# Two transformer blocks in one kernel: ScalarE's order at the block boundaries, and two gate units in the attention's last tiles

## The chip, the cores and the metric

The kernel runs on one core of a Trainium2 chip. The metric is device time in microseconds for one execution of the whole program. Three executions of the kernel before were timed; one further execution was profiled.

## The reference

Two blocks run one after the other on x of 256 tokens by 1024 channels, all in float32. The first is sparse and windowed attention beside a gated MLP, followed by a SwiGLU feed-forward. The second is a block with adaptive modulation: latent attention over chosen keys beside a state-space mixer (SSD), then a SwiGLU feed-forward.

```python
# first block
h = h + rms_norm(mixer(rms_norm(h, norm_mix_pre)), norm_mix_post)
h = h + rms_norm(swiglu_ffn(rms_norm(h, norm_ffn_pre)), norm_ffn_post)
# second block
mod = (silu(c) @ ada_w + ada_b)             # six rows of 1024: shift, scale and gate, twice
h = rmsnorm(x, pre_norm_mix) * (1.0 + scale_m) + shift_m
proj = h @ w_in                             # q_lat, kv_lat, k_idx, w_idx, z, xbc, dt, g_a, g_b
y_a = sparse_mla_attention(...) @ w_o_attn  # 16 heads, latent keys of 128
y_b = ssd_mixer(z, xbc, dt_raw, ...) @ w_o_ssd
mix = (sigmoid(g_a) * y_a + sigmoid(g_b) * y_b) @ w_out
x = x + gate_m * rmsnorm(mix, post_norm_mix)
h2 = rmsnorm(x, pre_norm_ffn) * (1.0 + scale_f) + shift_f
x = x + gate_f * rmsnorm((silu(u_gate) * u_up) @ w_ffn_out, post_norm_ffn)
```

## The kernel before

Every matrix product of float32 is made of three products of rounded parts: high times high, high times low, low times high. A weight unit of 128 partitions by 1024 numbers is loaded by SyncE into a ring of RING = 4 slots (`w_raw`). ScalarE copies it to its high part (`w_hi`, L870, in `split`), VectorE subtracts to get its low part (`w_lo`, L1357), and for some units GpSimd does the subtraction (L715). TensorE takes the units in order. `split_to(u)` on ScalarE or VectorE means: split all units up to u that are not split yet. A slot's high part can be rewritten once TensorE has used the unit before it (`unit_used`). All five queues are written out by hand, each engine works strictly in its own order, and semaphores tie them together.

The streams of weights that matter here, in order: `s_wo` (output of the first mixer), `s_gu` (first feed-forward, in), `s_dn` (its output), `s_lat` (latents of the second block), `s_z`, `s_z2` (z of the SSD), `s_ga` (gate g_a, 8 units), `s_oa` (attention output, 8 units), `s_xbc` (input of the convolution, 16 blocks of two units), and later `s_wo2`, `s_gu2`, `s_dn2`.

**The boundaries.** Between two parts x is updated and normalised again; there are three of them, `boundary(0)` after `s_wo`, `boundary(1, 0)` after `s_dn` and `boundary(2, 1)` after `s_wo2`. A product is made in two column halves. The last four units of the second half are done for token half 0 first, then for token half 1, so that token half 0 can be worked on meanwhile. For each token half t:

- ScalarE squares the product's halves (`square_m0` at L898, `square_m1` at L909) and takes the root (`root_m` at L913); the root needs a table load, which the one-column activation into `warm` (L959) brings forward.
- VectorE multiplies with the gain (`gained`, L1403), updates x (`new_x`, L1413), multiplies x with the next gain (`gain_x`, L1420).
- ScalarE squares x and takes the root (`square_x`, L920 to L924); VectorE makes a diagonal of the reciprocal (`rstd_x`, L1397 and L1398).
- TensorE turns x with that diagonal (`turn`, L2102, 8 products into banks 4 to 7).
- ScalarE reads the turned x in four pieces as high parts of h (`piece_hi`, L932 without a shift, L936 with one), VectorE makes the low parts (`piece_lo`, L1357 or L1432), and TensorE begins the next product for that token half, piece by piece (L2061 to L2063, or L2428 for the latents).

Four units of each next stream (v, v+1, v+2, v+3) are held in buffers of their own, since they are used once for each token half. The low part of v+3 is made by GpSimd, of the others by VectorE.

**The second attention.** It runs over NTILE = 32 tiles of 8 queries. Step n of the loop on TensorE makes the logits of tile n (L2493 to L2498), transposes the weights of tile n-2 (L2506), makes single pieces of z (`s_z2`, until step 24), and multiplies with the values for tile n-3 (L2520). In the last three steps only the latter parts are left. z's blocks are read on ScalarE by `read_z` (L1215), at steps 17 and 33. Behind the loop follow the per-head output matmuls (L2527), the cumulated sums for the SSD (L2534 to L2538), the gate's units into banks 0 to 3, and the attention output into banks 4 to 7:

```python
        pe.wait_ge(act_read, s_z2.act0 + s_z2.n)
        for c in range(2):
            if c == 1:
                pe.wait_ge(uv_lo, 2)
            for j in range(4):
                u = s_ga.u0 + 4 * c + j
                pe.wait_ge(lo_ready, u + 1)
                for t in range(TT):
                    ins = tm_half(u, 2 * j, t, bank[2 * c + t][:, :], h_hi, h_lo, j == 0, j == 3)
                ins.then_inc(unit_used, 1)
```

Through the gate's and the output's units VectorE also does `modulate`: 24 steps (L1481, L1484) that add silu(c) times a row block of `ada_w` (chunks 7 to 9 of 8 steps each) to an accumulator. GpSimd loads those rows by quarters of a chunk (L724), beginning when the per-head output matmuls are done; a quarter is loaded when VectorE has used the same quarter of the chunk before. TensorE sums the accumulators over partitions (`add_up`, L2152), ScalarE copies the sums (L1259), and GpSimd stores them (`store_sums`) and waits for the landing, between two low parts of `s_xbc` that it makes.

Of the kernel before, what the change touches and what calls it, by code (L numbers as in the profile page):

```python
# [26 lines left out]
ACT = mybir.ActivationFunctionType  # L27
# [4 lines left out]
TT = S // P  # L32
# [83 lines left out]
def _emit(nc, ctx, a, out):  # L116
# [418 lines left out]
    GB_READ = (4, 13)  # L535
    OS_STEPS = {KI - 2: 2, KI - 1: 2, KI: 4, KI + 1: 4}
# [310 lines left out]
    def _(act):  # L847
# [92 lines left out]
        def product_end(b):  # L940

            st = PRODUCTS[b]
            split_to(st.u0 + len(st.ks) + 3)
            square_m0(b, 0)
            split_to(st.u0 + len(st.ks) + 4)
            square_m0(b, 1)
            split_to(st.u0 + 2 * len(st.ks))

        def boundary(b, bias=None):
# [9 lines left out]
            act.activation(warm[:, 2 + b:3 + b], eps, ACT.Sqrt)  # L959
# [4 lines left out]
            if b != 1:  # L964
                square_m1(b, 1)
                root_m(b, 1)
            piece_hi(b, 0, 0, bias)
            piece_hi(b, 0, 1, bias)
            if b == 1:
                square_m1(b, 1)  # L970
                root_m(b, 1)
            split_to(v + 4)
# [252 lines left out]
        for n in range(NTILE + 2):  # L1225
# [16 lines left out]
            if n % 16 == 1 and n > 16:  # L1242
                read_z(s_z2, n // 16 - 1, 2 + 2 * s_z.n + 2 * (n // 16 - 1))
# [14 lines left out]
        act.wait_ge(sums_mm, 2)  # L1258
        act.activation(sums2[0:96, 0, :], bank[2][0:96, :], ACT.Copy).then_inc(sums_read, 1)  # L1259
        for b in range(s_xbc.n + 1):  # L1260
            if b < s_xbc.n:
# [85 lines left out]
    def _(dve):  # L1347
# [430 lines left out]
        for n in range(NTILE + 4):  # L1778
# [18 lines left out]
            if n % 8 in (2, 3) and n < NTILE:  # L1797
                split_half(s_z2.u0 + n // 8 + AHEAD, n % 8 - 2)
        for b in range(4):
# [17 lines left out]
        for b in range(4):  # L1817
            split_to(s_ga.u0 + 2 * b + 2 + AHEAD)
# [120 lines left out]
    def _(pe):  # L1939
# [546 lines left out]
        z2_tile = 0  # L2486
        for n in range(NTILE + 3):
# [21 lines left out]
            for _ in range(2 if n < 2 else 1 if n % 2 == 0 and z2_tile < 2 * KD else 0):  # L2509
# [3 lines left out]
                z2_tile += 1  # L2513
            if n >= 3:
# [7 lines left out]
                ins.then_inc(lt_pv, 1)  # L2522
        pe.wait_ge(uv_in, 16)
# [16 lines left out]
        pe.wait_ge(act_read, s_z2.act0 + s_z2.n)  # L2540
        for c in range(2):
            if c == 1:
                pe.wait_ge(uv_lo, 2)
            for j in range(4):
                u = s_ga.u0 + 4 * c + j
                pe.wait_ge(lo_ready, u + 1)
                for t in range(TT):
                    ins = tm_half(u, 2 * j, t, bank[2 * c + t][:, :], h_hi, h_lo, j == 0, j == 3)
                ins.then_inc(unit_used, 1)
# [11 lines left out]
        add_up(MOD_FIRST, MOD_SECOND, 2)  # L2561
        for b in range(2):
            fm_block(s_xbc, b, h_hi, h_lo)
        with pe.Fori(1, s_xbc.n // 4) as i:
# [145 lines left out]
```

## Time and profile before

| what | value |
|---|---|
| median of 3 runs | 956.2 us (955.8 to 957.12) |
| the profiled execution | 954.68 us |
| its span, first to last instruction | 953.0 us |
| TensorE busy | 938.7 us, 98% |
| VectorE busy | 662.6 us, 70% |
| ScalarE busy | 539.8 us, 57% |
| GpSimd busy | 233.6 us, 25% |
| read from HBM | 176.90 MB, 187 GB/s over the span |
| granted TensorE clock | 1.000 |

The difference between the profiled execution's time and its span (1.7 us) lies before the first and after the last instruction. Boundary 0 lies at 125 to 150 us of the span, boundary 1 at 321 to 344, the second attention at 416 to 484, the gate's and the attention output's units at 490 to 534, the convolution from 535 on, boundary 2 at 745 to 768. Idle time of an engine stands in brackets in a timeline, with what ended it; a busy TensorE is not one at its peak, since the ends of matmuls are modelled.

### The profile page before, as it was taken

The numbers are of one execution on the slowest core, as the hardware profiler recorded it, in microseconds if no ns is written. First come the engines' busy times: TensorE is split into PE (matmuls) and PEld (weight loads), VectorE is DVE, ScalarE is ACT, GpSimd is POOL, SyncE is SP. The second block draws the span as 40 slices with busy tenths as digits, with TensorE's granted clock in tenths as the row PEclk, the third lists the DMA queues.
The fourth block names the chain that finished last, engine by engine and source line by source line (L and its number), as shares of the span: only waits on it lengthen the run. The fifth ranks groups of instructions, "written<-read, shape, count | busy, mean of one in ns | idle before, by whom it ended". The sixth has DMA issues, their size and how long they took to land.

```text
span 953.0 us, 15383 instructions
## 1 busy us (share of the span) xinstructions
PE 938.7 (98%) x5665; PEld 801.9 (84%) x5665; DVE 662.6 (70%) x1098; ACT 539.8 (57%) x958; POOL 233.6 (25%) x235
## 2 busy tenths in 40 slices
PE   9999999999999999999999999999999999999997
PEld 8987887888887898999978899986688878888786
DVE  5776676777786668965678666678976767755453
ACT  6677675444535558744546456567764664544443
POOL 5304001111122150499922144320200101000100
PEclk9999999999999999999999999999999999999999
DMA  9765268788888714750149666651345778666561
GB/s 284 236 185 167 80 195 267 243 277 274 276 298 243 234 46 132 201 154 23 29 164 338 181 184 189 163 172 67 111 155 165 232 243 259 189 190 189 192 219 67
DMA packets 131352, 179.00 MB, mean 188 GB/s; under 512 B 8124, under 2 KB 96910, under 8 KB 131280
## 3 DMA queue, kind: packets, MB, share of 16 engines
q1 hardware_dynamic: 120384, 144.53, 48.3%
q0 software_dynamic: 10304, 33.18, 11.5%
q8 instruction: 44, 0.72, 0.3%
q10 hardware_dynamic: 592, 0.34, 0.1%
q14 instruction: 28, 0.23, 0.1%
HBM read 176.90 MB, written 1.12 MB: 187 GB/s over the span
## 4 chain that ended last, share of the span: by engine, by line
PE 86%; DVE 5%; ACT 5%; DMA 2%; issue 1%; POOL 1%; SPq 0%; DVEq 0%; ACTq 0%; POOLq 0%
PE bank L2061 17%; PE bank L2063 17%; PE bank L2062 16%; PE bank L1982 16%; PE bank L2497 1%; PE bank L2493 1%; PE bank L2520 1%; DVE w_lo L1357 1%; PE bank L2234 1%; PE bank L2013 1%; DMA w_raw<-in_w_in 1%; PE bank L2428 1%; PE bank L2116 1%; ACT w_hi L870 1%; PE bank L2102 1%
## 5 line engine op out<-in xcount | busy, mean ns | idle before, releaser
L1357 DVE TENSOR_TENSOR w_lo<-w_raw,w_hi 128x1024 fp32r<-128x1024 f32 (+1 forms) x243 | 284.5, 1192 | 75.8 <-ACT w_hi L870 75.3
L870 ACT ACTIVATE w_hi<-w_raw 128x1024 fp32r<-128x1024 f32 (+1 forms) x262 | 265.8, 1038 | 113.9 <-PE bank L2063 74.3
L2061 PE MATMUL bank<-w_hi,h_hi 128*128 128x512 f32 x448 | 179.0, 399 | 0.2 <-DVE h_lo L1357 0.2
L2063 PE MATMUL bank<-w_hi,h_lo 128*128 128x512 f32 x448 | 174.8, 390 | 0.0
L2062 PE MATMUL bank<-w_lo,h_hi 128*128 128x512 f32 x448 | 174.3, 389 | 0.0
L1982 PE MATMUL bank<-h_hi,w_hi 128*128 128x256 f32 x432 | 124.5, 288 | 1.4 <-DVE h_lo L1520 1.1
L1982 PE MATMUL bank<-h_lo,w_hi 128*128 128x256 f32 x432 | 122.1, 283 | 0.0
L1982 PE MATMUL bank<-h_hi,w_lo 128*128 128x256 f32 x432 | 122.1, 283 | 0.0
L2061 PE MATMUL bank<-w_hi,ff_hi 128*128 128x512 f32 x272 | 107.6, 395 | 0.3
L2062 PE MATMUL bank<-w_lo,ff_hi 128*128 128x512 f32 x272 | 106.0, 390 | 0.0
L2063 PE MATMUL bank<-w_hi,ff_lo 128*128 128x512 f32 x272 | 105.9, 389 | 0.0
L2063 PEld LDWEIGHTS bank<-w_hi,h_lo 128*128 128x128 f32 x448 | 84.1, 188 | 18.0
L2061 PEld LDWEIGHTS bank<-w_hi,h_hi 128*128 128x128 f32 x448 | 84.2, 188 | 16.2 <-issue 0.6
L2062 PEld LDWEIGHTS bank<-w_lo,h_hi 128*128 128x128 f32 x448 | 84.3, 188 | 15.8
L715 POOL TENSOR_TENSOR w_lo<-w_raw,w_hi 128x1024 fp32r<-128x1024 f32 x27 | 65.2, 2414 | 117.7 <-DVE w_lo L1357 94.2
L1982 PEld LDWEIGHTS bank<-h_hi,w_hi 128*128 128x128 f32 x432 | 82.7, 192 | 3.1 <-DVE w_lo L1357 1.5
L1982 PEld LDWEIGHTS bank<-h_lo,w_hi 128*128 128x128 f32 x432 | 82.8, 192 | 0.0
L1982 PEld LDWEIGHTS bank<-h_hi,w_lo 128*128 128x128 f32 x432 | 82.7, 191 | 0.0
L724 POOL DMA_DIRECT2D ada_raw<-in_ada_w x48 | 34.4, 718 | 188.3 <-DVE ada_acc L1484 175.6
L1484 DVE SCALAR_TENSOR_TENSOR ada_acc<-ada_raw,c_silu,ada_acc 128x512 f32<-128x512 f32 x84 | 63.0, 750 | 4.0 <-DVE ada_acc L1484 0.5
L816 POOL TENSOR_SCALAR ff_hi<-pos_f,own_pos 128x256 fp32r<-128x256 f32 x64 | 64.2, 1018 | 3.5 <-PE bank L2498 3.5
L997 ACT ACTIVATE silu_tok<-bank 128x256 f32<-128x256 f32 x44 | 16.9, 384 | 81.5 <-PE bank L2063 81.4
(463 smaller groups left out, 1634.3 us busy)
## 6 DMA issues: line engine op xcount, KB each, us to landing
w_raw<-in_w_in SPq DMA_DIRECT2D x84, 512.0 KB, 3.8
ada_raw<-in_ada_w POOLq DMA_DIRECT2D x48, 512.0 KB, 6.2
w_raw<-in_w_gate_up SPq DMA_DIRECT2D x88, 256.0 KB, 5.2
w_raw<-in_w_ffn_in SPq DMA_DIRECT2D x88, 256.0 KB, 3.9
w_raw<-in_w_down SPq DMA_DIRECT2D x22, 512.0 KB, 6.3
w_raw<-in_w_ffn_out SPq DMA_DIRECT2D x22, 512.0 KB, 4.3
w_raw<-in_w_out SPq DMA_DIRECT2D x16, 512.0 KB, 3.7
w_raw<-in_w_o_ssd SPq DMA_DIRECT2D x16, 512.0 KB, 3.5
```

The costliest lines, as they stand in the source:

```text
L715: pool.tensor_tensor(low(u, n), w_raw[:, u % RING, 0:n], high(u, n).bitcast(F32), ALU.subtract).then_inc(lo_ready, 1)
L724: pool.dma_start(ada_raw[:, j, :].rearrange("p (k c) -> p k c", k=2), ada[:, 2 * j:2 * j + 2, 512 * MOD_CHUNKS[c]:512 * MOD_CHUNKS[c] + 51 ...
L816: ins = pool.tensor_scalar(reached[:, n % 2, c, :], pos_f[:, 0:S], own_pos[:, 2 * n + c:2 * n + c + 1], None, ALU.is_ge)
L870: act.activation(high(u, n), w_raw[:, u % RING, 0:n], ACT.Copy).then_inc(hi_ready, 1)
L997: act.activation(silu_tok[:, b % 2, t, :], bank[2 * (b % 2) + t][:, 0:256], ACT.Silu).then_inc(gu_silu, 1)
L1357: return dve.tensor_tensor(dst, src, hi.bitcast(F32), ALU.subtract)
L1484: ins = dve.scalar_tensor_tensor(acc, src, c_silu[:, k:k + 1], acc, ALU.mult, ALU.add)
L1982: ins = pe.matmul(out_b[:, s, :], w[:, kk, c], x[:, k0 + k, :], start=k == 0 and s == 0 and step == 0, stop=k == sum(st.ks) - 1 and s == 1 ...
L2013: ins = pe.matmul(out_b[:, t, 0:ncol], x[:, k, c], w[:, kk, :], start=first, stop=end and last and t == 1, skip_group_check=True)
L2061: pe.matmul(out, x_hi[:, k, x], hi, start=start, stop=False, skip_group_check=True)
L2062: pe.matmul(out, x_hi[:, k, x], lo, start=False, stop=False, skip_group_check=True)
L2063: return pe.matmul(out, x_lo[:, k, x], hi, start=False, stop=stop, skip_group_check=True)
```

## The change

Eight edits are made.

1. In `product_end(0)`, on ScalarE, the activation into `warm` that loads the root's table stands before the unit `s_wo.u0 + 6`; the one in `boundary` remains for boundary 1 alone. (In boundary 2 the table is already the right one.)
2. In `boundary` on ScalarE the order is now the same for all three: squares of x for token half 0, the held unit v+3, pieces 0 and 1, square and root of token half 1, pieces 2 and 3. Before, boundaries 0 and 2 had square and root first, pieces 0 and 1, the held unit, pieces 2 and 3; boundary 1 had pieces 0 and 1, square and root, the held unit, pieces 2 and 3.
3. The second block of z is read at step 29 in place of step 33.
4. The gate's unit 0 is done in two halves, in steps 32 and 33 of the attention's loop, between the transposes and the values; its unit 1 directly behind the loop; the other six where all eight stood.
5. ScalarE and VectorE split the gate's units 2 and 3 before they read the per-head outputs.
6. VectorE splits two more units ahead of each group of three modulation steps in the gate's part.
7. TensorE does `add_up` of chunks 7 to 9 behind the first two blocks of `s_xbc`, in place of before them.
8. ScalarE copies these sums at the third turn of its convolution loop, in place of before the loop.

```diff
+    Z2_READ = (17, 29)
@@ ScalarE, product_end
+            if b == 0:
+                split_to(st.u0 + len(st.ks) + 2)
+                act.activation(warm[:, 2:3], eps, ACT.Sqrt)
             split_to(st.u0 + len(st.ks) + 3)
@@ ScalarE, boundary
             split_to(v + 2)
-            act.activation(warm[:, 2 + b:3 + b], eps, ACT.Sqrt)
+            if b == 1:
+                act.activation(warm[:, 3:4], eps, ACT.Sqrt)
             square_m1(b, 0)
             root_m(b, 0)
             split_to(v + 3)
             square_x(b, 0)
-            if b != 1:
-                square_m1(b, 1)
-                root_m(b, 1)
+            split_to(v + 4)
             piece_hi(b, 0, 0, bias)
             piece_hi(b, 0, 1, bias)
-            if b == 1:
-                square_m1(b, 1)
-                root_m(b, 1)
-            split_to(v + 4)
+            square_m1(b, 1)
+            root_m(b, 1)
             piece_hi(b, 0, 2, bias)
@@ ScalarE, second attention
-            if n % 16 == 1 and n > 16:
-                read_z(s_z2, n // 16 - 1, 2 + 2 * s_z.n + 2 * (n // 16 - 1))
+            if n in Z2_READ:
+                b = Z2_READ.index(n)
+                read_z(s_z2, b, 2 + 2 * s_z.n + 2 * b)
+        split_to(s_ga.u0 + 4)
@@ ScalarE, convolution
-        act.wait_ge(sums_mm, 2)
-        act.activation(sums2[0:96, 0, :], bank[2][0:96, :], ACT.Copy).then_inc(sums_read, 1)
         for b in range(s_xbc.n + 1):
+            if b == 2:
+                act.wait_ge(sums_mm, 2)
+                act.activation(sums2[0:96, 0, :], bank[2][0:96, :], ACT.Copy).then_inc(sums_read, 1)
@@ VectorE
+        split_to(s_ga.u0 + 4)
         for b in range(4):
             dve.wait_ge(uv_hi, b + 1)
@@ VectorE
-            split_to(s_ga.u0 + 2 * b + 2 + AHEAD)
+            split_to(s_ga.u0 + 2 * b + 4 + AHEAD)
             for step in range(3 * b, 3 * b + 3):
@@ TensorE
+        def ga_half(c, j, t):
+
+            u = s_ga.u0 + 4 * c + j
+            if t == 0:
+                pe.wait_ge(lo_ready, u + 1)
+            ins = tm_half(u, 2 * j, t, bank[2 * c + t][:, :], h_hi, h_lo, j == 0, j == 3)
+            if t == TT - 1:
+                ins.then_inc(unit_used, 1)
+
         for n in range(NTILE + 3):
@@ TensorE, between the transposes (and z) and the values of a step
+            if n in (NTILE, NTILE + 1):
+                if n == NTILE:
+                    pe.wait_ge(act_read, s_z2.act0 + s_z2.n)
+                ga_half(0, 0, n - NTILE)
@@ TensorE, behind the loop
+        for t in range(TT):
+            ga_half(0, 1, t)
         pe.wait_ge(uv_in, 16)
@@ TensorE, behind the cumulated sums
-        pe.wait_ge(act_read, s_z2.act0 + s_z2.n)
         for c in range(2):
             if c == 1:
                 pe.wait_ge(uv_lo, 2)
-            for j in range(4):
-                u = s_ga.u0 + 4 * c + j
-                pe.wait_ge(lo_ready, u + 1)
+            for j in range(2 - 2 * c, 4):
                 for t in range(TT):
-                    ins = tm_half(u, 2 * j, t, bank[2 * c + t][:, :], h_hi, h_lo, j == 0, j == 3)
-                ins.then_inc(unit_used, 1)
+                    ga_half(c, j, t)
@@ TensorE, convolution
-        add_up(MOD_FIRST, MOD_SECOND, 2)
         for b in range(2):
             fm_block(s_xbc, b, h_hi, h_lo)
+        add_up(MOD_FIRST, MOD_SECOND, 2)
```

## Rows read from the trace of the kernel before

**Rows 1.** The page: busy us, share of the span and count, first engines.

```profile
PE 938.7 (98%) x5665; PEld 801.9 (84%) x5665; DVE 662.6 (70%) x1098; ACT 539.8 (57%) x958; POOL 233.6 (25%) x235
```

**Rows 2.** TensorE's waits: us in total, times, longest.

```profile
PE bank L2102 <- DVE rstd L1398: 2.4, 3, 0.9
```

**Rows 3.** Timeline, boundary 0: start us, us, engine, what, idle before and its releaser.

```profile
125.03 1.06 ACT L870 ACTIVATE w_hi<-w_raw 128x1024 fp32r<-128x1024 f32 x1 [1.37 <-PE bank L2063]
...
131.83 2.36 DVE L1357 TENSOR_TENSOR ff_lo<-w_raw,ff_hi 128x1024 fp32r<-128x1024 f32 x2 [0.17 <-ACT ff_hi L870]
...
132.71 0.39 PE L2063 MATMUL bank<-w_hi,h_lo 128*128 128x512 f32 x1
...
132.76 1.28 ACT L959 ACT_TABLE_LOAD   x1
...
134.17 0.58 ACT L909 ACTIVATE var_sd<-bank 128x512 f32<-128x512 f32 x1
...
138.15 0.39 PE L2063 MATMUL bank<-w_hi,h_lo 128*128 128x512 f32 x1
...
139.25 2.02 PE L2102 MATMUL bank<-rstd,mT 128*128 128x128 f32 x16 [0.71 <-DVE rstd L1398]
...
141.88 2.38 POOL L715 TENSOR_TENSOR ff_lo<-w_raw,ff_hi 128x1024 fp32r<-128x1024 f32 x1 [44.27 <-ACT ff_hi L870]
...
142.93 1.90 DVE L1413 SCALAR_TENSOR_TENSOR x_tok<-mT,st,x_tok 128x512 f32<-128x512 f32 x1
...
147.65 2.02 PE L2102 MATMUL bank<-rstd,mT 128*128 128x128 f32 x16 [0.92 <-DVE rstd L1398]
```

**Rows 4.** Timeline, boundary 1.

```profile
332.78 1.14 ACT L936 ACTIVATE h_hi<-bank,shift 128x128 fp32r<-128x128 f32 x4 [1.38 <-PE bank L2102]
...
334.73 0.88 ACT L870 ACTIVATE lat_hi<-w_raw 128x832 fp32r<-128x832 f32 x1
...
336.91 0.35 PE L2428 MATMUL bank<-lat_hi,h_hi 128*128 128x256 f32 x1 [1.07 <-DVE h_lo L1432]
...
337.40 1.46 DVE L1413 SCALAR_TENSOR_TENSOR x_tok<-mT,st,x_tok 128x512 f32<-128x512 f32 x2
...
340.59 0.29 DVE L1398 TENSOR_SCALAR rstd<-mats,st 128x128 f32<-128x128 f32 x1
```

**Rows 5.** Timeline, boundary 2.

```profile
750.05 0.39 PE L2063 MATMUL bank<-w_hi,h_lo 128*128 128x512 f32 x1
...
750.47 0.60 ACT L909 ACTIVATE var_sd<-bank 128x512 f32<-128x512 f32 x1 [0.30 <-PE bank L2063]
...
756.84 1.12 ACT L936 ACTIVATE h_hi<-bank,shift 128x128 fp32r<-128x128 f32 x4
...
758.23 0.47 PE L2061 MATMUL bank<-ff_hi,h_hi 128*128 128x512 f32 x1 [0.38 <-DVE h_lo L1432]
...
760.69 1.25 DVE L1413 SCALAR_TENSOR_TENSOR x_tok<-mT,st,x_tok 128x512 f32<-128x512 f32 x1
...
764.77 2.02 PE L2102 MATMUL bank<-rstd,mT 128*128 128x128 f32 x16 [0.81 <-DVE rstd L1398]
```

**Rows 6.** Timeline of TensorE, the second attention's last tiles.

```profile
481.13 0.44 PE L2506 MATMUL bank<-mats,isc 128*128 128x128 f32 x2 [0.31 <-DVE isc L1789]
481.54 0.71 PE L2520 MATMUL bank<-work,kv 128*128 128x128 f32 x4
...
484.13 3.67 PE L2527 MATMUL bank<-oT,work 128*64 128x256 f32 x32 [0.47 <-DVE oT L1794]
```

**Rows 7.** The loads of ada_w and a pair of low parts; last, the loads' us to landing.

```profile
488.25 2.93 POOL L724 DMA_DIRECT2D ada_raw<-in_ada_w  x4 [9.45 <-PE bank L2527]
...
514.26 2.36 DVE L1357 TENSOR_TENSOR w_lo<-w_raw,w_hi 128x1024 fp32r<-128x1024 f32 x2 [2.10 <-ACT w_hi L870]
...
DMA to landing us min/median/max: 4.3/6.2/7.3
```

**Rows 8.** Timeline of TensorE in the convolution, a unit's first matmul.

```profile
561.08 0.38 PE L1982 MATMUL bank<-h_hi,w_hi 128*128 128x256 f32 x1
```

## The prediction, made before the changed kernel was run

> **What bounds the kernel now.** I read the page's busy times first: TensorE is busy 938.7 of 953.0 us [rows 1], so neither another engine nor the transfers can be what the whole kernel waits for; the change can only win what TensorE still loses in gaps. Then the list of TensorE's waits, longest in total first [rows 2]: on top is the turn of x at the boundaries (L2102), behind the diagonal that VectorE makes at L1398. Then the timeline around each boundary, around the end of the second attention, and through the gate's and the attention output's units. The ends of matmuls are modelled, so I go by starts: 24 matmuls of 512 columns, the second token half of a product, lie between 132.71 and 138.15, 0.227 us each [rows 3], and one is shown as 0.39 us long. A gap is therefore the idle time that the row shows plus 0.16 us: 0.71 + 0.16 = 0.87 us and 0.92 + 0.16 = 1.08 ahead of the two turns of boundary 0 [rows 3]; 1.07 + 0.16 = 1.23 inside boundary 1 [rows 4]; 0.38 + 0.17 = 0.55 ahead of 758.23 and 0.81 + 0.16 = 0.97 ahead of 764.77 in boundary 2 [rows 5].
>
> **Boundary 0, the root table.** The last matmul of the first token half starts at 132.71; ScalarE is then in the table load (132.76, 1.28 us), warms the table (0.1 us more, since it overlaps), and squares the half only at 134.17 [rows 3]. In boundary 2, whose table is in place, the same square starts 0.42 us after the same matmul (750.05 to 750.47) [rows 5]. With the load moved up it starts at 132.71 + 0.42 = 133.13. Not all of that 1.04 us reaches the turn: VectorE splits two units from 131.83 for 2.36 us [rows 3], and takes up the half only behind them; from 134.87, a short wait after the square, to 134.15. So the first turn comes 0.72 us earlier, at 138.5, with 0.15 us of gap left. The load now stands ahead of the unit whose high part starts at 125.03 after 1.37 us of idle time [rows 3]: load and warming are 1.4 us, so it slips by at most 0.1 us, and its low part, done at 127.4, is only reached around 130.2. Cost nothing; without that cover 1.4 us.
>
> **Boundaries 0 and 2, the held unit.** Its high part (1.05 us) and the square and root of the second half (1.02 us) change places; the unit now stands before the first pieces of h. There ScalarE is free: from the end of x's squares until the first transposes are through, 0.72 us after the turn begins (332.06 to 332.78 in boundary 1, 1.38 us idle [rows 4]). Boundary 0: free from 137.85, unit to 138.9, pieces at 138.5 + 0.72 = 139.2; nothing lost, and pieces 2 and 3 keep their place. Boundary 2: unit 755.15 to 756.2, pieces at 755.82 + 0.72 = 756.54 in place of 756.84, TensorE at 757.95 in place of 758.23 [rows 5]: 0.28 us.
> What matters more stands on GpSimd. It makes this unit's low part and starts when the high part is there: at 141.88, 2.38 us [rows 3], and in boundary 2 the same way. VectorE's first update of x falls inside it and takes 1.90 us (142.93) and 1.25 us (760.69); in boundary 1, hardly disturbed, two together take 1.46 us [rows 3 to 5]. After the change GpSimd runs at about 139.6 to 142.0 and 756.9 to 759.3 and is done before the update starts, at 142.5 and 760.4; what VectorE does in between reads PSUM and was not slower beside GpSimd before. From the update's start to a possible turn I take boundary 1: 337.40 to the diagonal's end at 340.88, and 0.15, make 3.6 us [rows 4]. Boundary 0: second turn at 142.5 + 3.6 = 146.1 in place of 147.65, 1.5 us in all, the first turn's share included (TensorE itself is ready at about 145.85). Boundary 2: 760.43 + 3.6 = 764.05 in place of 764.77, with everything 0.65 us. Bounds: if the update stays as slow, only 0.72 and 0.28 remain, less 0.1 for the later second square; above, the whole gaps, 1.95 and 1.5.
> The Trainium skill (SBUF — State Buffer, Who interferes with whom) gives a reason: a VectorE instruction with two SBUF inputs and a GpSimd one that reads SBUF exclude each other, and the later one blocks until the other ends. The trace agrees: the update of 142.93 ended at 144.83, 0.57 us after GpSimd at 144.26. By that rule the update runs at full speed once GpSimd is done, which is my sum; were the slowness of another kind, boundaries 0 and 2 would give 0.9 us together in place of 2.15.
>
> **Boundary 1.** Square and root stood between the pieces already, and the unit (0.88 us, 334.73) behind them, so that pieces 2 and 3 came late and TensorE stood still for 1.23 us [rows 4]. The unit goes into the 1.38 us before 332.78 and ends at 332.3. Pieces 2 and 3 start 0.8 us earlier, and TensorE with them. The diagonal of the second half moves along (340.88 to 340.1), ahead of TensorE's need at 340.45. 0.8 us; below 0.5, if some returns at the second turn; above 1.2.
>
> **The end of the second attention.** The last tiles leave gaps: 0.31 + 0.16 = 0.47 us at 481.13, which stays, since it is ahead of transposes behind which the new work stands; 0.47 + 0.17 = 0.64 us at 484.13; and, start to start, 0.14 us ahead of 481.54 and some 0.4 us in like pieces behind it [rows 6]. Four half units of 6 matmuls (1.36 us each, moved and not added) fill all but the first. Each change of kind costs about 0.1 us, so of 1.2 us I count 0.8; bounds 0.5 and 1.1. The bank needs z's last read, moved on ScalarE from behind the loop to step 29, where 0.6 us fits into the 0.96 us of idle time of a step; units 2 and 3 of the gate are split ahead of the attention's output, where both engines stood idle for 1.9 us.
>
> **What comes later.** The output matmuls (L2527) and the sums behind them start some 4.7 us later than before, and GpSimd's loads of ada_w wait for the former (488.25, now about 492.9) [rows 7]. VectorE finishes the cumulated parts at 498.0 in place of 493.3, but has two units fewer ahead. From there: a pair of units takes 2.28 us (514.26 to the steps behind it) [rows 7], three steps of modulation 2.3, a chunk's products with the gate 1.2. I walked that chain against TensorE's 2.72 us a unit from 494.8. Tightest: the output product's unit 4 (low part 521.4, wanted 522.0), unit 6 (527.0 against 527.5), and the first quarter of chunk 9 (landed about 522.7, wanted 523.4, by the median of 6.2 us to landing [rows 7]). Half a microsecond of slack each, so 0, and this is a rival below. The sums of the modulation move behind two blocks of the convolution: the same matmuls, no gain of their own, but GpSimd's queue (low parts, the store of the sums with a wait for its landing, low parts again) gets that much more room, and the gap at 561.08 goes, 0.34 us behind the start of the matmul before it where the pace is 0.12 [rows 8]. ScalarE's copy of the sums (0.6 us) now stands before the third block's splits, which are wanted 4 us later.
>
> **The sum.** 1.5 + 0.8 + 0.65 + 0.8 + 0.2 = 3.95 us. Behind each place TensorE sets its own pace and the others follow its marks, so nothing should swallow it. The profiled execution took 954.68 us for a span of 953.0; it would take 950.7. The median of the runs shown is 1.5 us above it: 956.2 - 4.0 = 952.2 us.
>
> **The rivals.** *Half of it* (0.20): the updates of x stay slow for another reason, or a second turn finds its next limit: 0.9 + 0.6 + 0.6 = 2.1 us, 954.1 us. *No change* (0.17): the gains come but are lost again in the tight chain on VectorE; a stall of 2 to 4 us there leaves 954.3 to 956.2, say 955.2. *Slower* (0.06): VectorE's backlog. It is in order; where it waits for a quarter of ada_w, the low parts behind wait too. A quarter is only loaded when the same quarter of the chunk before is used, so a start 4.7 us later and two loads in a row at the worst landing seen, 7.3 us in place of 6.2 [rows 7], put it late by up to 6.9 us. From 0.5 us on TensorE pays, from 4.5 us on the change loses; 6.9 us would give 956.2 - 4.0 + 6.4 = 958.6. Against it: VectorE had time to spare in that chain, 2.10 us at 514.26 alone [rows 7]. *More* (0.05): all gaps go, 6 us, 950.2.
>
> **How the numbers follow.** The likeliest case (0.52) is 952.2, with its own range 951.2 to 953.6. 0.2% is 1.9 us and about what a measurement tells from no change; faster is 0.52 + 0.20 + 0.05 = 0.77, same 0.17, slower 0.06. The range 950.8 to 955.0 leaves out the slower case, part of the unchanged one and the end of the larger gain.
>
> **What would show it.** Right: the first turn of boundary 0 within 0.2 us of the product's last matmul; all updates of x at L1413 near 0.75 us; no wait at L2428; between the last tiles only one gap, ahead of the transposes; no wait of L2061 for a low part through the attention output. Wrong: a gap near 1 us still ahead of the second turns; TensorE waiting for w_lo between 495 and 540 us, with VectorE idle behind ada_raw; the table load in the way of a split.

## The result, and the profile after

The changed kernel took 950.34 us (median of 6 runs, 949.83 to 950.92) beside 956.16 us for the kernel before (median of 6 runs on the same chip, 954.55 to 957.12): a ratio of 0.9942, with a 95% interval of 0.993 to 0.9953. It is faster, by more than the forecast said: 952.2 us was forecast, and the range began at 950.8. The profiled execution took 950.07 us for a span of 948.4 us, 4.6 us less than the span of before.

The page's busy line and the list of TensorE's waits, us in total, times and longest:

```profile
PE 937.6 (99%) x5665; PEld 801.2 (84%) x5665; DVE 659.5 (70%) x1098; ACT 539.0 (57%) x957; POOL 233.7 (25%) x235
```

```profile
PE bank L2163 <- POOL wsT L663: 1.1, 1, 1.1
PE bank L1987 <- DVE h_lo L1524: 0.9, 1, 0.9
PE bank L2107 <- DVE rstd L1402: 0.5, 2, 0.3
PE bank L2521 <- DVE isc L1793: 0.3, 1, 0.3
```

The turn of x, which stood on top of this list before [rows 2], now waits 0.5 us in place of 2.4 (L2107 is the same line as L2102 before). The two rows above it are of the kernel's first 12 us.

The timeline at boundary 0, to be read beside [rows 3]: first ScalarE's square, then both turns, GpSimd's subtraction and VectorE's pair of updates.

```profile
132.83 0.60 ACT L910 ACTIVATE var_sd<-bank 128x512 f32<-128x512 f32 x1 [0.39 <-PE bank L2068]
...
138.17 2.02 PE L2107 MATMUL bank<-rstd,mT 128*128 128x128 f32 x16
...
139.34 2.39 POOL L716 TENSOR_TENSOR ff_lo<-w_raw,ff_hi 128x1024 fp32r<-128x1024 f32 x1 [42.03 <-DVE ff_lo L1361]
...
141.80 1.41 DVE L1417 SCALAR_TENSOR_TENSOR x_tok<-mT,st,x_tok 128x512 f32<-128x512 f32 x2
...
145.49 1.95 PE L2107 MATMUL bank<-rstd,mT 128*128 128x128 f32 x16
```

Neither turn has an idle time in brackets (the 8 products of a turn show as 16 records). GpSimd is through at 141.73, 0.07 us before the updates begin, and two of them take 1.41 us where one took 1.90.

Boundary 1, beside [rows 4]: the second held unit of the latents on ScalarE, the table load behind it, the first turn, a product with the latents and the second turn. Boundary 2, beside [rows 5]: both turns. The end of the attention, beside [rows 6]: the transposes, and the per-head output matmuls.

```profile
322.86 1.06 ACT L871 ACTIVATE lat_hi<-w_raw 128x1024 fp32r<-128x1024 f32 x1 [1.58 <-DMA w_raw<-in_w_in]
323.94 1.28 ACT L964 ACT_TABLE_LOAD   x1
...
330.43 2.02 PE L2107 MATMUL bank<-rstd,mT 128*128 128x128 f32 x16 [0.26 <-DVE rstd L1402]
...
334.50 0.36 PE L2433 MATMUL bank<-lat_hi,h_hi 128*128 128x256 f32 x1 [0.28 <-DVE h_lo L1436]
...
338.66 1.96 PE L2107 MATMUL bank<-rstd,mT 128*128 128x128 f32 x16
...
478.67 0.44 PE L2521 MATMUL bank<-mats,isc 128*128 128x128 f32 x2 [0.31 <-DVE isc L1793]
...
486.09 3.67 PE L2548 MATMUL bank<-oT,work 128*64 128x256 f32 x32
...
752.04 2.02 PE L2107 MATMUL bank<-rstd,mT 128*128 128x128 f32 x16
...
760.16 2.02 PE L2107 MATMUL bank<-rstd,mT 128*128 128x128 f32 x16 [0.28 <-DVE rstd L1402]
```

The wait inside boundary 1 is 0.28 us in place of 1.07, but a new one of 0.26 us stands ahead of its first turn. Behind the last tiles no wait is left but that ahead of the transposes.

TensorE runs one fixed sequence, so the starts of its six turns cut both executions into the same pieces. The first piece begins with the first matmul of the mixer's output product (115.25 us before, 114.94 after). All lengths are differences of start times, in us; "forecast" is the prediction's term.

| piece | before | after | difference | forecast |
|---|---|---|---|---|
| to boundary 0's second turn | 32.40 | 30.55 | -1.85 | -1.5 |
| from there to boundary 1's first turn | 184.41 | 184.94 | +0.53 | 0 |
| between boundary 1's turns | 9.03 | 8.23 | -0.80 | -0.8 |
| from there to boundary 2 (attention, gate, convolution) | 414.73 | 413.38 | -1.35 | -1.0 |
| between boundary 2's turns | 8.95 | 8.12 | -0.83 | -0.65 |
| behind | 188.23 | 188.24 | 0 | 0 |

With the 0.31 us ahead of 115 us that makes 4.6 us. The four pieces that the change reaches give 4.83 us, against 3.95 forecast. The second line, which it does not reach, gave 0.53 us back in this execution.

### The profile page after: what moved, and what is told of

The parts are those of the page before. It is cut to its first block, busy times and chain, and to the rows that moved or that the text cites. A ratio compares the mean times of both kernels' runs of the same rounds, so it can differ in the third digit from the quotient of the medians.

```text
span 948.4 us, 15382 instructions
## 1 busy us (share of the span) xinstructions
PE 937.6 (99%) x5665; PEld 801.2 (84%) x5665; DVE 659.5 (70%) x1098; ACT 539.0 (57%) x957; POOL 233.7 (25%) x235
## 4 chain that ended last, share of the span: by engine, by line
PE 88%; DVE 4%; ACT 3%; DMA 2%; issue 1%; POOL 0%; SPq 0%; DVEq 0%; ACTq 0%
PE bank L1987 18%; PE bank L2066 16%; PE bank L2068 16%; PE bank L2067 16%; PE bank L2512 1%; DMA w_raw<-in_w_in 1%; PE bank L2508 1%; DVE w_lo L1361 1%; PE bank L2539 1%; PE bank L2239 1%; PE bank L2018 1%; PE bank L2220 1%; PE bank L2433 1%; DMA w_raw<-in_w_down 1%; PE bank L2121 1%
## 5 line engine op out<-in xcount | busy, mean ns | idle before, releaser
L2066 PEld LDWEIGHTS bank<-w_hi,ff_hi 128*128 128x128 f32 x272 | 51.1, 188 | 14.2 <-DVE w_lo L1361 2.6
```

The costliest lines, as they stand in the source:

```text
L2066: pe.matmul(out, x_hi[:, k, x], hi, start=start, stop=False, skip_group_check=True)
```

## The experiments

Three questions were open: which part earns what, whether the reasons given for each are the true ones, and how much of the 5.8 us between the first medians is the change.

| run | median us (runs) | ratio to before, 95% interval | profiled: us, span |
|---|---|---|---|
| kernel before again (e0) | 954.85 (10) | 1.0006 [0.9995, 1.0016] | 954.9, 953.2 |
| edits 1 and 2 (e1) | 951.8 (5) | 0.9965 [0.9952, 0.9979] | 951.8, 950.1 |
| edit 2 (e2) | 952.43 (6) | 0.9966 [0.9954, 0.9978] | 952.76, 951.0 |
| edits 3 to 8 (e3) | 954.39 (11) | 0.9995 [0.9986, 1.0004] | 953.64, 951.9 |
| changed again (e4) | 950.23 (5) | 0.9943 [0.993, 0.9957] | 949.55, 947.8 |
| GpSimd held back (e5) | 951.86 (4) | 0.9955 [0.994, 0.997] | 953.33, 951.6 |
| two moves more (e6) | 950.57 (5) | 0.9937 [0.9924, 0.9951] | 950.65, 948.9 |
| edits 7 and 8 (e7) | 955.2 (10) | 0.9996 [0.9986, 1.0005] | 955.0, 953.3 |
| edit 1 (e8) | 954.37 (10) | 0.999 [0.998, 0.9999] | 953.65, 951.9 |
| three moves more (e9) | 948.97 (5) | 0.9928 [0.9915, 0.9942] | 948.81, 947.0 |
| without edits 5 and 6 (e10) | 956.84 (10) | 1.0011 [1.0002, 1.002] | 956.69, 955.0 |
| changed a third time (e11) | 951.28 (5) | 0.9951 [0.9937, 0.9964] | 951.3, 949.6 |

The kernel before ran beside them with medians of 954.99 (e0 to e3, 22 runs), 955.64 (e4 to e7, 15 runs) and 955.64 us (e8 to e11, 21 runs).

And the same pieces as above, in us:

| run | to boundary 0's 1st, 2nd turn | to boundary 1 | between its turns | to boundary 2 | between its turns |
|---|---|---|---|---|---|
| before | 24.00, 32.40 | 184.41 | 9.03 | 414.73 | 8.95 |
| e0 | 24.00, 32.41 | 184.51 | 8.94 | 414.79 | 8.95 |
| e8 (edit 1) | 23.26, 31.76 | 184.07 | 8.96 | 414.81 | 8.93 |
| e2 (edit 2) | 24.00, 31.34 | 184.73 | 8.16 | 414.83 | 8.13 |
| e1 (edits 1, 2) | 23.24, 30.57 | 184.60 | 8.23 | 414.85 | 8.13 |
| e7 (edits 7, 8) | 24.00, 32.41 | 185.14 | 8.94 | 414.39 | 8.95 |
| e3 (edits 3 to 8) | 23.97, 32.37 | 184.68 | 8.94 | 413.50 | 8.94 |
| after | 23.23, 30.55 | 184.94 | 8.23 | 413.38 | 8.12 |
| e4 (all) | 23.24, 30.58 | 183.99 | 8.16 | 413.41 | 8.13 |
| e11 (all) | 23.26, 30.60 | 185.57 | 8.24 | 413.69 | 8.15 |
| e5 (GpSimd late) | 23.25, 31.63 | 186.54 | 8.24 | 413.41 | 8.63 |
| e6 (two more) | 23.24, 30.56 | 184.44 | 8.14 | 412.91 | 8.13 |
| e9 (three more) | 23.25, 30.57 | 184.16 | 8.16 | 412.94 | 7.71 |
| e10 (no 5, 6) | 23.25, 30.57 | 184.41 | 8.16 | 420.13 | 8.15 |

All columns but the third repeat to within some 0.1 us (once 0.3) in kernels that are alike there. The third, 184 us of the first feed-forward, lies between 183.99 and 186.54 and does not follow the edits. The medians alone do not carry the small parts: the intervals of e3 and e7 reach over 1, and that of e8 ends at 0.9999. What a part is worth is read from these pieces, of one profiled execution for each kernel.

### The parts, one by one: e0 to e3, e7, e8

Edits 1 and 2 in e1, edit 2 in e2, edit 1 in e8, all on the kernel before. Edit 2 is:

```diff
             square_x(b, 0)
-            if b != 1:
-                square_m1(b, 1)
-                root_m(b, 1)
+            split_to(v + 4)
             piece_hi(b, 0, 0, bias)
             piece_hi(b, 0, 1, bias)
-            if b == 1:
-                square_m1(b, 1)
-                root_m(b, 1)
-            split_to(v + 4)
+            square_m1(b, 1)
+            root_m(b, 1)
```

> The kernel before once more. The ratio is 1 within 0.1%. Its trace shows where an execution near the median of 956.2 us loses what the first profiled one (954.68 us) did not: by theory B at boundary 1, where ScalarE waits for the second latent unit's landing (0.3 to 1.5 us more ahead of the first turn there); by theory C in the last tiles of the attention or the convolution; by a third, at the very beginning, before the first matmul, where it has nothing to do with the change.

> The kernel before with edits 1 and 2 alone (root table and order on ScalarE at the boundaries). Theory A (TensorE's gaps add up as the two traces show them): boundary 0 gives 1.9 us, boundary 1 0.4 to 0.8, boundary 2 0.8, together 3.1 to 3.5 us less than the kernel before, in the profile and in the median. Theory B (typical executions of the kernel before lose some 1.2 us more than its profiled one, at a place that the boundaries' order mends): 4.3 to 4.7 us in the median and 3.1 to 3.5 in the profile. Theory C (the extra 1.2 us come from the attention's end and the convolution): 3.1 to 3.5 us here in both.

> Edit 2 alone (the held unit before the pieces of h, the root table where it was). If the update of x at boundary 0 was slow because of GpSimd's low part, the second turn's gap there closes without the table's move, and only the first turn's 0.7 us stays: 2.3 to 2.8 us less than the kernel before, updates of x all near 0.75 us. If the table's move is what freed the second half too, 1.2 to 1.6 us.

> Edit 1 alone (boundary 0's table load ahead of a split), on the kernel before. The order of edit 2 alone left the first turn's gap of boundary 0 (0.87 us) and closed the second one. Theory A (the first turn waits for ScalarE behind the table load, the second for the updates that GpSimd slows): here it is the other way round, the first turn comes 0.7 to 0.85 us earlier and the second, whose update of x still runs beside GpSimd's subtraction, keeps a gap near 1.1 us or more, since GpSimd moves along; 0.7 us in all at most, 954.6 us beside 955.3. Rival: the first turn's wait is not the load's, and its gap stays at 0.87; nothing then, 955.3.

Edits 3 to 8 in e3, 7 and 8 alone in e7:

> Edits 3 to 8 alone (gate units in the attention's end, splits, the sums' place). Theory A: 1.05 us at the attention's end and 0.25 at the convolution, 1.3 us less than the kernel before, in profile and median. Theory C: 2.5 us in the median. Rival (the chain on VectorE stalls in some executions): under 1 us, with waits of TensorE for w_lo between 495 and 540 us.

> Edits 7 and 8 alone (the sums of the modulation behind two blocks of the convolution, and ScalarE's copy of them at its third turn), on the kernel before. Theory A: the gap of 0.25 us at 561 us goes and nothing else moves, 954.7 us beside 955.0, which no measurement tells from no change; the gaps of the attention's last tiles stay as they were, so that the 1.1 us that edits 3 to 8 took from the span belong to the gate's units but for these 0.25. Rival: the sums that come later find a bank or GpSimd's queue occupied, a wait of 0.3 us or more beside L2152 or ahead of the convolution's low parts, and the span is not shorter.

The parts add up: edits 1 and 2 take 1.84 us at boundary 0 (32.41 to 30.57), 0.7 to 0.8 at boundary 1 and 0.82 at boundary 2, and nothing further on; edits 3 to 8 take 1.3 us between boundaries 1 and 2 and nothing elsewhere. Of these, 7 and 8 have 0.35 to 0.4, and the rest, 0.9 to 1.0, is the attention's end; edits 3 to 6 were not run one by one. e0 was also to show where an execution of 956 us loses time that the first profiled one did not; its profiled execution took 954.9 us, so that stays open.

Nearly all of the 0.35 to 0.4 us of edits 7 and 8 lies at the gap of [rows 8]. TensorE's matmuls just ahead of it and just behind it, in the kernel before:

```profile
560.74 0.28 PE L1982 MATMUL bank<-h_hi,w_lo 128*128 128x256 f32 x1
...
561.30 0.28 PE L1982 MATMUL bank<-h_lo,w_hi 128*128 128x256 f32 x1
```

Two starts are late, not one: 561.08 comes 0.34 us behind 560.74, and 561.30 comes 0.22 us behind 561.08, where the pace is 0.12. That makes 0.32 us here and 0.38 in e0, which has the same gap (560.90, 561.29, 561.52). In e7 the pace does not break there.

What the two edits of boundary 0 do apart shows best who waits for whom. The turns of x with edit 2 alone, then with edit 1 alone, with GpSimd's subtraction and VectorE's updates beside it:

```profile
139.65 2.02 PE L2098 MATMUL bank<-rstd,mT 128*128 128x128 f32 x16 [0.71 <-DVE rstd L1394]
...
140.82 2.41 POOL L715 TENSOR_TENSOR ff_lo<-w_raw,ff_hi 128x1024 fp32r<-128x1024 f32 x1 [42.78 <-DVE ff_lo L1353]
...
143.28 1.41 DVE L1409 SCALAR_TENSOR_TENSOR x_tok<-mT,st,x_tok 128x512 f32<-128x512 f32 x2
```

```profile
138.47 2.02 PE L2106 MATMUL bank<-rstd,mT 128*128 128x128 f32 x16
...
141.19 2.40 POOL L715 TENSOR_TENSOR ff_lo<-w_raw,ff_hi 128x1024 fp32r<-128x1024 f32 x1 [43.59 <-ACT ff_hi L870]
...
142.23 2.56 DVE L1417 SCALAR_TENSOR_TENSOR x_tok<-mT,st,x_tok 128x512 f32<-128x512 f32 x2
...
146.97 2.02 PE L2106 MATMUL bank<-rstd,mT 128*128 128x128 f32 x16 [0.85 <-DVE rstd L1402]
```

Edit 1 (the table load) frees the first turn and leaves the second a wait of 0.85 us, 0.92 before; edit 2 leaves the first turn's 0.71 us and brings the pair of updates from 2.57 us (the kernel before, run again) to 1.41. Alone they are worth 0.65 and 1.07 us there, together 1.84, 0.12 more than the sum: two waits, each with its own cause.

### Is it GpSimd? e5

```diff
+        pool.wait_ge(m_sd, 2)
         split(pool_held[0])
...
+        pool.wait_ge(m_sd, 6)
         split(pool_held[2])
```

> The changed kernel, with GpSimd waiting in boundaries 0 and 2 for the root of the product's second token half before it makes its low part (2.39 us). In boundary 0 that is at about 140.6 us in place of 139.34, so that it runs until 143.0, over the start of VectorE's second pair of updates of x (141.80). Theory A (the updates were slow because GpSimd was at its subtraction at the same time): the pair takes 2.5 to 2.8 us in place of 1.41, its end moves from 143.2 to 144.4, the second turn starts 1.0 us behind TensorE's last matmul, and in boundary 2 the gap of 0.44 us grows to about 1.0; together 1.6 us, 952.0 us, half of the gain of the boundaries gone. Rival (the updates gained by their place behind other work on VectorE or ScalarE, and GpSimd has nothing to do with it): the pair stays at 1.4 us and the time at 950.4, within 0.2 us.

Nothing but the time of GpSimd's subtraction is moved, and of what stands behind it in GpSimd's queue, and the old rows are back. GpSimd, the updates and the second turn of boundary 0, in this kernel, and boundary 2's second turn:

```profile
140.80 2.40 POOL L716 TENSOR_TENSOR ff_lo<-w_raw,ff_hi 128x1024 fp32r<-128x1024 f32 x1 [43.46 <-ACT st L916]
...
141.84 2.57 DVE L1419 SCALAR_TENSOR_TENSOR x_tok<-mT,st,x_tok 128x512 f32<-128x512 f32 x2
...
146.58 2.02 PE L2109 MATMUL bank<-rstd,mT 128*128 128x128 f32 x16 [0.86 <-DVE rstd L1404]
...
763.40 2.02 PE L2109 MATMUL bank<-rstd,mT 128*128 128x128 f32 x16 [0.79 <-DVE rstd L1404]
```

The pair starts 1.36 us before GpSimd is through (143.20) and takes 1.16 us longer than 1.41. In boundary 2 the overlap is 0.70 us (759.32 to 760.02) and the pair takes 1.91 us, 0.50 longer. GpSimd's instruction takes 2.40 us in both, so the loss follows the overlap, not GpSimd's whole duration. By the pieces the wait costs 1.05 us at boundary 0 and 0.50 at boundary 2, 1.55 us in all, as expected; the median rose by 1.6 (950.23 to 951.86), but by only four runs. The theory stands, its rival falls. (e5 also has the longest first feed-forward, 186.54 us; whether GpSimd's later queue has a part in that was not tested.)

The Trainium skill (SBUF — State Buffer, Who interferes with whom) says that such a pair of instructions shares a lock, held by the earlier one until it ends. The two losses above agree with it, each 0.2 us short of the overlap.

### Do the splits have to move along? e10

```diff
-        split_to(s_ga.u0 + 4)          # ScalarE, VectorE
...
-            split_to(s_ga.u0 + 2 * b + 4 + AHEAD)
+            split_to(s_ga.u0 + 2 * b + 2 + AHEAD)
```

> The changed kernel without edits 5 and 6: units 2 and 3 of the gate are split behind the per-head outputs, and VectorE only two units ahead of its modulation, as before the change. Theory A (the gate's earlier units only pay because the splits moved along): VectorE reaches the low part of unit 2 behind its cumulated parts, at 494.7 us, and TensorE wants it at 491.5; it stands still for about 4.5 us, the changed kernel loses all its drain gain and more, 954.8 us. Rival (VectorE has room enough and edits 5 and 6 are ornament): within 0.3 us of 950.3.

The low parts of units 2 and 3 on VectorE, and TensorE's restart:

```profile
495.18 2.36 DVE L1360 TENSOR_TENSOR w_lo<-w_raw,w_hi 128x1024 fp32r<-128x1024 f32 x2
...
496.46 0.79 PE L2064 MATMUL bank<-w_hi,h_hi 128*128 128x512 f32 x1 [4.34 <-DVE w_lo L1360]
...
498.33 0.63 PE L2065 MATMUL bank<-w_lo,h_hi 128*128 128x512 f32 x1
...
502.12 0.39 PE L2064 MATMUL bank<-w_hi,h_hi 128*128 128x512 f32 x1
```

The stall is there, 4.50 us by starts, but the stretch to boundary 2 grew by 6.7 us (413.41 to 420.13). The windows of the stretch ahead of the restart, of the one behind it, and of the next (core 0; from, to, length, busy us and count of TensorE, its weight loads, VectorE, ScalarE and GpSimd, granted clock, DMA share, GB/s):

```profile
494.00:496.40 2.40, 0.00 (x0) 0.00 (x0) 2.30 (x5) 1.36 (x2) 0.00 (x0) 0.54 1.00 336
496.50:500.90 4.40, 4.40 (x11) 3.43 (x12) 4.26 (x6) 0.00 (x0) 0.72 (x1) 0.50 0.94 322
501.50:506.00 4.50, 4.50 (x22) 3.70 (x21) 2.51 (x4) 1.64 (x3) 1.45 (x2) 1.00 0.92 320
```

After the 4.34 us of idling TensorE goes on at a granted clock of 0.50, that is 1.2 of 2.4 GHz: ten matmuls from 496.46 to 500.89 take 0.44 us each in place of 0.227, 2.2 us more. So edits 5 and 6 are worth 6.7 us in this execution, not the 4.5 expected, and 5.6 us between the medians (956.84 and, for e11 on the same chip, 951.28); without them the whole change ends a little behind the kernel before (ratio 1.0011, from 1.0002 up). The lower stretch may not come in every execution: seven of the ten runs have a mean granted clock of 0.995 or 0.996 and take 956.3 to 958.7 us, three have 0.998 and take 955.8 to 956.2; only one of the seven was profiled. VectorE's place in the queue decided, as expected; the rival falls. e10 takes both edits away at once. The stall is at a unit that edit 5 splits earlier; whether edit 6 is needed too is not shown.

### Is the gain 4.6 or 5.8? e4, e11

> The changed kernel once more, since the size of the gain is in question: 5.8 us between the medians first measured, 4.6 us between the spans of the two profiled executions, 2.9 and 1.1 us from the two parts run alone. Theory A (the gain is the sum of the gaps that the two profiled executions show, and the median of the runs before stood 1 us above that kernel's usual time): 955.0 - 4.6 = 950.4 us, ratio 0.995. Theory B (the whole does more than its parts): ratio 0.994 again, 949.2 us beside a kernel before at 955.0. In the gaps: none ahead of the turns of boundary 0, 0.4 us at most ahead of boundary 1's first turn if the second unit of the latents lands at 322.8 us or later, and none there if it lands by 322.

> The changed kernel a third time, on the same chip as the version above, so that their medians can be set side by side, and for one more profiled execution: the sum of the places with no late landing is 1.95 + 0.8 + 0.83 + 1.35 + about 0.3 at the start = 5.2 us. Theory A: the median lies 5.0 us, give or take 0.5, below the kernel before; its profiled execution shows boundary 0's second turn at 145.5 to 146.1 us and 8.15 to 8.25 us between the two turns of boundary 1. Rival (the gain is 4.6 or less and the first measurement was fortunate): 4.0 to 4.6 us.

The ratio came out at 0.9943 and 0.9951, after 0.9942. All 64 runs of the kernel before that stood beside a changed one, on several chips, have a median of 955.5 us, the 16 runs of the changed kernel 950.7: 4.8 us, close to what the four pieces add up to (4.83). Neither theory was quite right. The differences of medians are 5.8, 5.4 and 4.4 us, the last one in the range of e11's rival; single medians lay from 0.5 us below to 0.7 us above these two.

Most of the spread between the three profiled executions of the changed kernel (spans of 948.4, 947.8 and 949.6 us) sits in the 184 us of the first feed-forward; the rest is ahead of the first piece and, in e11, 0.3 us on the way to boundary 2. The feed-forward ends with ScalarE's high part of the latents' second unit and the first turn of boundary 1; the rows of the changed kernel stand above, here are the former in e11, then both in e5:

```profile
323.72 1.07 ACT L871 ACTIVATE lat_hi<-w_raw 128x1024 fp32r<-128x1024 f32 x1 [1.40 <-DMA w_raw<-in_w_in]
```

```profile
325.54 1.06 ACT L873 ACTIVATE lat_hi<-w_raw 128x1024 fp32r<-128x1024 f32 x1 [2.20 <-DMA w_raw<-in_w_in]
...
333.12 2.02 PE L2109 MATMUL bank<-rstd,mT 128*128 128x128 f32 x16 [0.88 <-DVE rstd L1404]
```

The turn came 7.57 to 7.59 us behind that start in all three (322.86 to 330.43, 323.72 to 331.31, 325.54 to 333.12). In the kernel before it was 7.57 as well (324.49 to 332.06), with a gap of 0.06 us only: TensorE itself was not done with the matmuls ahead of the turn until 332.00, 2.0 us later than after the change (330.01). In e4 the transfer took 4.0 us in place of 6.9 and the turn had no wait. The rest of the spread stands a little earlier, where TensorE waits for a split of w_down: 0.40 us at 294.73 after, 0.98 us in two places in e11, 1.20 us at 299.52 in e5, nothing in e4; in e11 ScalarE had waited 2.48 us for a transfer of w_down just ahead of them.

### A version that goes further: e6, e9

e6 changes two things in the changed kernel, and e9 has a third.

```diff
@@ ScalarE, boundary
-            split_to(v + 2)
             if b == 1:
+                split_to(v + 1)
                 act.activation(warm[:, 3:4], eps, ACT.Sqrt)
+            split_to(v + 2)
@@ TensorE, step n: ahead of the transposes, and ahead of the values
+            if n == NTILE:
+                pe.wait_ge(act_read, s_z2.act0 + s_z2.n)
+                ga_half(0, 0, 0)
...
-            if n in (NTILE, NTILE + 1):
...
+            if n == NTILE + 1:
+                ga_half(0, 0, 1)
@@ VectorE, boundary (e9)
             rstd_m(b, 1)
-            piece_lo(b, 0, 3, bias)
+            if b == 1:
+                piece_lo(b, 0, 3, bias)
             new_x(b, 1, 0)
             new_x(b, 1, 1)
+            if b != 1:
+                piece_lo(b, 0, 3, bias)
```

> The changed kernel with two moves more. In boundary 1 the table load stands before the second held unit of the latents in place of behind it; ScalarE waits 1.58 us for that unit's transfer, so the load (1.4 us with its warming) falls into the wait and the square of the product starts at 324.0 in place of 325.35. And the two halves of the gate's first unit stand ahead of the transposes (step 32) and ahead of the values (step 33). Theory A (both gaps are waits of the kind named): the gap of 0.42 us ahead of boundary 1's first turn closes, and so does that of 0.48 us ahead of the transposes at 478.67, 0.8 to 0.9 us in all, 949.6 us. Rival 1: the values of the tile, now only behind the transposes, wait for ScalarE's copy of them and the gap comes back there, 0.4 us of the second gain lost: 950.0 us. Rival 2: at boundary 1 VectorE, not ScalarE, is the last before the turn (its own split of the unit that landed late stands ahead), and nothing closes: 950.4 us.

> The kernel with the table load of boundary 1 ahead of the late unit and the gate's half unit ahead of the transposes, and one move more: in boundaries 0 and 2 VectorE updates x of token half 1 ahead of the last low piece of token half 0 (0.61 us in boundary 2) in place of behind it. TensorE wants that piece at 758.3 us, and it would be done by 758.1. Theory A (boundary 2's second turn stands at the end of VectorE's chain, the gap of 0.44 us being this piece's place): the gap closes, 0.44 us; with 0.48 us ahead of the transposes and up to 0.4 us at boundary 1 it takes 1 to 1.3 us off the changed kernel, 949.2 us beside 950.3, unless the granted clock dips somewhere. Rival: the piece now comes too late for TensorE's fourth unit and the gap opens there, so that this move gives nothing or costs 0.3 us: 949.8.

Two of the three work. The stretch to boundary 2 is 412.94 us in place of 413.41 (412.91 in e6), and boundary 2's 7.71 in place of 8.13. The end of the attention and the second turn of boundary 2 in e9:

```profile
477.62 0.47 PE L2070 MATMUL bank<-w_hi,h_hi 128*128 128x512 f32 x1
...
479.09 0.38 PE L2528 MATMUL bank<-mats,isc 128*128 128x128 f32 x2
479.31 0.61 PE L2544 MATMUL bank<-work,kv 128*128 128x128 f32 x4
...
755.11 1.41 DVE L1418 SCALAR_TENSOR_TENSOR x_tok<-mT,st,x_tok 128x512 f32<-128x512 f32 x2
756.43 0.60 DVE L1437 SCALAR_TENSOR_TENSOR h_lo<-bank,shift,h_hi 128x128 fp32r<-128x128 f32 x2
...
758.78 2.02 PE L2111 MATMUL bank<-rstd,mT 128*128 128x128 f32 x16
```

No brackets on TensorE: the half unit covers the wait ahead of the transposes, the values behind them wait for nothing, and the last low piece, done at 757.03, is early enough. e9 took 948.97 us, all five runs below 949.5, and is 0.7% faster than the kernel before; beside the changed kernel on the same chip (951.28) that is 2.3 us, of which the two moves explain 0.9; in the profiled executions another 1.4 us is the 184 us stretch (184.16 against 185.57). The third move stays open: in e6 and e9 the latents' unit was not late enough for the old order to lose anything. By the 7.57 us above, e6's first turn (331.56) would have had no wait with its unit there at 323.80 either.

e6's median, 950.57, hides its gain. Its profiled execution lost 1.5 us at 98.5 us, and only there, by the granted clock:

```profile
98.50:102.10 3.60, 3.60 (x18) 3.40 (x17) 0.00 (x0) 0.00 (x0) 0.00 (x0) 0.53 0.30 113
```

(The columns are those of the windows above; 16 matmuls of 256 columns came every 0.213 us in place of 0.119.) No other profiled execution shows such a stretch there. Its five times fall in two groups, 948.8 and 949.16 against 950.57 to 950.65, which is the same 1.5 us; that the dip makes the groups was not tested, and the mean granted clocks do not tell (0.999 and 1.0 in the faster two, 0.998 to 0.999 in the others).

## Why the prediction missed, point by point

**The likeliest case was the one that came**, mechanism by mechanism, but its terms were too small and its base too high. The step that failed is the sum: "1.5 + 0.8 + 0.65 + 0.8 + 0.2 = 3.95 us", of which the pieces measured 4.83, with every term but boundary 1's too small. From the profiled execution's own time, as the prediction first wrote it, 4.83 would have given 954.68 - 4.83 = 949.85 us; it was 950.07.

- *Boundary 0, 1.5 us: it was 1.85.* The first turn came 0.77 us earlier (0.72 forecast) and the square at 132.83, as its step said (133.13, less the 0.31 us by which this execution was ahead). The failed term is "done before the update starts, at 142.5", 4.0 us behind the first turn at 138.5. No row is given for it: the update followed the turn by 3.63 us (138.17 to 141.80) as it had before the change (139.25 to 142.93, 3.68). With that, the prediction's own figures allow the second turn at 138.5 + 3.6 + 3.6 = 145.7, ahead of TensorE's own "about 145.85", which gives 1.8 us. From the update 3.43 us lead to the diagonal's end, as forecast (3.48), and TensorE itself became the limit. "The whole gaps" was the upper bound given (1.95); it is nearly what came.
- *Boundary 1, 0.8 us: right*, 1.23 us of gap down to 0.44, 0.80 between the turns. What the prediction did not see is ahead of it: the first turn hung on a late transfer with 0.06 us to spare, so that of the 2 us by which TensorE came earlier, a late landing takes some back (0.42 us after, 0.26 in e11, 1.04 in e5, nothing in e4). One of its signs of being right did not come either: a wait at the latents' product stayed, 0.28 us at L2433 (L2428 before).
- *Boundary 2, 0.65 us: it was 0.83.* Its own figures gave 0.72 (764.05 for 764.77), and the sum took 0.65. The gap ahead of the second turn went from 0.97 to 0.44, and that ahead of 754.17 from 0.55 to 0.28.
- *The updates of x: right*, and shown by e5. The rival "half of it" needed another reason for their slowness; the pair takes 1.41 us with GpSimd's subtraction out of the way and 2.57 us with it back, so none is left.
- *The end of the attention, 0.8 us: 0.9 to 1.0*, near the upper bound of 1.1. "Each change of kind costs about 0.1 us" took off too much.
- *The sums of the modulation, 0.2 us: 0.35 to 0.4.* Only the first late start of the gap at 561 us was priced (0.34 - 0.12 = 0.22); the start behind it, 0.1 us late as well, was left out.
- *The tight chain on VectorE, 0: right.* TensorE waits for nothing between 486 and 540 us in the changed kernel, in three profiled executions. e10 shows that edits 5 and 6 together hold it. The chain was as tight as it was said, though; the low parts of the attention output's units 4 and 5, and then 6 and 7, on VectorE, and TensorE's first matmul of unit 4:

```profile
517.87 2.35 DVE L1361 TENSOR_TENSOR w_lo<-w_raw,w_hi 128x1024 fp32r<-128x1024 f32 x2
...
519.41 0.39 PE L2066 MATMUL bank<-w_hi,ff_hi 128*128 128x512 f32 x1
...
523.19 2.35 DVE L1361 TENSOR_TENSOR w_lo<-w_raw,w_hi 128x1024 fp32r<-128x1024 f32 x2
```

  One of a pair takes 1.22 us, so unit 4's was done at 519.09, 0.32 us ahead of TensorE (0.6 forecast), and unit 6's at 524.41, 0.47 us ahead of 524.88 (0.5 forecast). The rivals "no change" and "slower" did not come.

**The base.** "The median of the runs shown is 1.5 us above it: 956.2 - 4.0." The three runs lay 0.7 us above the median of the 64 (955.5), and six runs of the changed kernel 0.35 us below their own (950.7). The distance of 1.9 us between forecast and first result is thus some 0.85 us of terms, 0.7 of base and 0.35 of chance. No one of the three would have carried the time out of the range: with the measured terms on the prediction's base it is 956.2 - 4.83 = 951.4 us, with its own terms on the base of 955.5 it is 951.6. The range began at 950.8 because the case "more" had only 0.05; four terms (boundaries 0 and 2, the attention's end, the sums) came out low together, and that was not allowed for.

## What to carry to other kernels

Where several small gaps close by the same kind of move, price each at the closed gap, up to where the pace is regular again, and take off only what a row shows; a cautious rounding in every term added up to 0.88 of 4.83 us here. Make the sum against the profiled execution, and give a median of three runs a microsecond of doubt of its own. Work moved into a wait only pays if what it consumes is moved too: without its splits this change lengthened the stretch to boundary 2 by 5.4 us in place of shortening it by 1.35.

## What the hardware showed beside that

- A stall's price does not end with it. After 4.34 us of idling, TensorE ran 4.4 us at the lower of its two clocks, and the stall of 4.5 us cost 6.7 (e10). The Trainium skill (TensorE: Matmul & The Clock Gate, What's actually happening) tells of a clock of 1.2 GHz after idling in place of 2.4; the trace agrees (0.50). The gaps of up to 1.2 us in the other kernels (0.87, 1.08 and 1.23 before, 1.20 in e5) are followed by no such stretch.
- The granted clock can also dip where the rows show TensorE busy throughout ahead of it (e6, 0.53 over 3.6 us from 98.5 on; 1.00 from 95 to 98.5). What set it off stays open.
- The same 512 KB transfer, that of the latents' second unit, took 4.0 us to land in e4 (issued at 315.83), 6.9 us in the first profiled execution of the changed kernel (315.95) and 7.5 us in e5 (318.02). The turn behind it waited 0.42, 0.26 and 0 us in three executions of the same kernel: such a step is on the critical path in some executions and not in others.
